# The lower weight parts that fall due while the scan runs, issued behind the scan's work of that step

## The reference, cut to what matters

```python
z, xbc, dt_f, dt_b, q, k, v, gates = split_cols(h @ w_in, IN_SPLITS)
...
seg = a_cum[:, :, :, None] - a_cum[:, :, None]
decay = jnp.exp(jnp.where(lower[:, :, None, None], seg, -jnp.inf)).astype(dtype)
cb = jnp.einsum('bclgn,bcsgn->bclsg', c_c, b_c)
y_diag = jnp.einsum('bclsg,bclsgr,bcsgrp->bclgrp', cb, decay, x_c)
...
y_off = jnp.einsum('bclgn,bcgrpn,bclgr->bclgrp', c_c, h_in, jnp.exp(a_cum).astype(dtype))
...
v = (y * jax.nn.silu(z)).astype(jnp.float32).reshape(b, s, SSD_GROUPS, d // SSD_GROUPS)
...
k, v = jnp.split(mem_n @ w_kv, 2, axis=-1)
```

## Time and profile before

| | |
|---|---|
| median of three runs | 2353.67 us (2353.35 to 2355.12) |
| the profiled execution's own time | 2353.92 us |
| its span, first to last instruction | 2352.1 us |
| busy: TensorE (PE) / its weight loads (PEld) | 2324.1 us / 2014.4 us |
| busy: VectorE (DVE) / ScalarE (ACT) / GpSimd (POOL) | 1636.3 / 1243.7 / 262.4 us |
| chain that ended last: share of PE / DVE / ACT | 93% / 3% / 2% |
| granted TensorE clock | 0.999 |

### The profile page before, as it was taken

How to read it: one execution, slowest core, us unless ns; L and a number is a source line. 1 busy time by engine, 2 the same in 40 slices (tenths; PEclk the granted TensorE clock), 3 DMA queues, 4 the chain that set the end, 5 groups by cost and what they waited for, 6 DMA issues and landing times.

```text
span 2352.1 us, 35281 instructions
## 1 busy us (share of the span) xinstructions
PE 2324.1 (99%) x14088; PEld 2014.4 (86%) x14088; DVE 1636.3 (70%) x2353; ACT 1243.7 (53%) x2026; POOL 262.4 (11%) x208
## 2 busy tenths in 40 slices
PE   8999999999999999999999999999999999999998
PEld 7778778777788888899988899998887888899997
DVE  5698845478865455687785788785677565777784
ACT  7777765346663344455554555554544354555552
POOL 0000000465100100100002200001122201100002
PEclk9999999999999999999999999999999999999999
DMA  6221236324666232233233233223322232333222
GB/s 200 81 73 52 88 103 206 103 95 121 204 214 213 88 118 75 81 116 100 90 99 110 86 119 108 90 81 113 110 64 63 90 117 72 108 108 106 87 76 91
DMA packets 177844, 254.05 MB, mean 108 GB/s; under 512 B 10000, under 2 KB 101392, under 8 KB 177680
## 3 DMA queue, kind: packets, MB, share of 16 engines
q1 hardware_dynamic: 176528, 250.22, 33.1%
q10 hardware_dynamic: 1152, 1.57, 0.2%
HBM read 233.93 MB, written 16.78 MB: 107 GB/s over the span
## 4 chain that ended last, share of the span: by engine, by line
PE 93%; DVE 3%; ACT 2%; issue 1%; DMA 0%; POOL 0%; DVEq 0%; SPq 0%; POOLq 0%
PE bank L1492 92%; DVE wlo L2523 1%; PE bank L1660 1%; ACT whi L1899 0%; PE bank L1683 0%; PE bank L1781 0%; PE bank L1805 0%; DVE T L2531 0%; DVE W L2523 0%; DMA zb<-scr_z 0%; ACT E L2163 0%; DVE bank L2842 0%; DMA raw<-in_w_in 0%; PE bank L1618 0%; DVE xg L2527 0%
## 5 line engine op out<-in xcount | busy, mean ns | idle before, releaser
L1492 PE MATMUL bank<-xopr,shi 128*128 128x256 f32 x3360 | 605.0, 283 | 0.0
L1492 PEld LDWEIGHTS bank<-xopr,shi 128*128 128x128 f32 x3360 | 524.5, 192 | 0.5
L1492 PE MATMUL bank<-xopr,slo 128*128 128x256 f32 x1680 | 475.4, 283 | 0.0
L2523 DVE TENSOR_TENSOR wlo<-raw,whi 128x1024 fp32r<-128x1024 f32 (+2 forms) x286 | 354.6, 1244 | 140.8 <-ACT whi L1899 140.2
L1492 PE MATMUL bank<-xh,whi 128*128 128x512 f32 x1016 | 408.0, 402 | 7.4 <-DVE wlo L2523 7.4
L1492 PE MATMUL bank<-xh,wlo 128*128 128x512 f32 x1016 | 397.5, 391 | 0.0
L1492 PE MATMUL bank<-xl,whi 128*128 128x512 f32 x1016 | 397.2, 391 | 0.0
L1899 ACT ACTIVATE whi<-raw 128x1024 fp32r<-128x1024 f32 (+2 forms) x286 | 292.8, 1031 | 136.1 <-PE bank L1492 121.0
L1492 PEld LDWEIGHTS bank<-xopr,slo 128*128 128x128 f32 x1680 | 322.5, 192 | 0.0
L1492 PEld LDWEIGHTS bank<-xh,whi 128*128 128x128 f32 x1016 | 191.5, 188 | 50.0 <-DVE wlo L2523 8.2
L1492 PEld LDWEIGHTS bank<-xh,wlo 128*128 128x128 f32 x1016 | 191.1, 188 | 41.6
(11 more groups left out here) (398 smaller groups left out, 4320.7 us busy)
## 6 DMA issues: line engine op xcount, KB each, us to landing
raw<-in_w_in SPq DMA_DIRECT2D x92, 512.0 KB, 3.5
quarter<-in_w_ffn_in SPq DMA_DIRECT2D x32, 512.0 KB, 4.5
quarter<-in_ffn_gate SPq DMA_DIRECT2D x32, 512.0 KB, 3.6
quarter<-in_ffn_up SPq DMA_DIRECT2D x32, 512.0 KB, 4.6
raw<-in_ffn_down SPq DMA_DIRECT2D x28, 512.0 KB, 4.2
raw<-in_w_xattn_kv SPq DMA_DIRECT2D x16, 512.0 KB, 4.5
raw<-in_w_kv_mem SPq DMA_DIRECT2D x16, 512.0 KB, 4.9
raw<-in_w_branch_ssd SPq DMA_DIRECT2D x16, 512.0 KB, 4.6
```

The lines of the kernel that those rows point to most:

```text
L1492: return e.matmul(out, l, r, start=start, stop=stop, skip_group_check=skip)
L2523: return e.tensor_tensor(out, a, b, op)
```

## The change

`point()` no longer writes the lower parts of weights while the scan runs. It returns them, and `run_beside` writes them at its own end, behind the generators, so behind the half step of the scan that is written at the same m. In `settle` and `drain` they are written directly behind the point. The other delayed steps keep their place, and outside the scan nothing is different.

```diff
+        behind_scan = [False]
+
         def point():
             due = [d for d in delayed if d[0] == 0]
             delayed[:] = [[d[0] - 1, d[1]] for d in delayed if d[0]]
+            if behind_scan[0]:
+                held = [d[1] for d in due if d[1][0] == "w_lo"]
+                due = [d for d in due if d[1][0] != "w_lo"]
+            else:
+                held = []
             for d in sorted(due, key=lambda d: d[1][0] not in ("w_lo", "s_lo")):
...
+            return held
...
         def run_beside(share):
 
-            point()
+            held = point()
             clock[0] += share
...
                     if next(g[0], "end") == "end":
                         beside.remove(g)
+            for what in held:
+                step(*what)
...
             if g in beside:
                 for _ in g[0]:
-                    point()
+                    for what in point():
+                        step(*what)
                 beside.remove(g)
...
             drain(scan)
+            behind_scan[0] = False
...
         scan = start(ssd(), 3.6)
+        behind_scan[0] = True
```

## The result

| | before | after |
|---|---|---|
| median of 16 executions each | 2353.9 us | 2357.47 us |
| ratio, 95% interval | | 1.0015 (1.0008 to 1.0021) |
| the profiled execution's own time / span | 2353.92 / 2352.1 us | 2357.18 / 2354.9 us |
| mean granted TensorE clock of it | 0.999 | 0.998 |

The changed kernel is 3.6 us slower, inside the 0.2% that I had called hardly measurable, and 0.5 us above my range; with this many executions the interval lies wholly above 1, so the change did make it slower. (One execution of each kernel took over 3800 us; neither moves its median by more than 0.2 us.) The other fifteen executions of the changed kernel go with their mean granted clock: five at 0.999 took 2354.1 to 2355.8 us, ten at 0.998 or 0.997 took 2357.2 to 2360.1 us. Lines of the changed kernel lie 14 further down.

What follows compares the result with a forecast made beforehand. TensorE was taken to bound the scan too, so only its waits could be won or made. Gains of -2.6 and a loss of +2.1 us gave -0.5 us, a median of 2353.2 us, range 2349.5 to 2357.0 us.

Steps and rivals of the forecast that it cites:

- the other moved parts I carry at 0: Remaining moved lower parts: room for 2 to 3 us more in z, so 0; at most 2.1 us a place otherwise.
- place 2: Wait of 1.94 us at 529.68 goes, but the lower part then delays bank 5's mask: -1.1 us, bounds -0.7 and -1.5.
- Place 1: TensorE's waits at 508.06 and 517.58 us for an exponential go: -0.5 and -0.2 us.
- Place 3: Wait of 1.84 us at 590.58 for the last `z_silu` goes, ScalarE is late next: -0.8 us, bounds -0.5 and -1.8.
- The gate: Near 635 us `wlo9` falls behind VectorE's wait for a z tile: +4.35 new wait, -1.21 and -1.00 returned, net +2.1 us.
- the lead is swallowed: Rival, 26%: later events on VectorE, ScalarE or transfers take back every gain, only the loss stays: 2355.8 us.
- slower: Rival, 12%: at the gate with the late z tile, gains gone and neither old wait returned: +4.35 us, 2358.0 us.
- wrong: Profile sign: if waits for E stay near 6.8 us in all, the mask was not what the lower part held up.

Runs made afterwards that it cites:

- only_82_84: Kernel before with only the lower parts of 549.12 and 566.66 us moved behind the scan's half step; median +2.4 us against the kernel before.
- all_but_96: Changed kernel with the lower part of 629.11 us put back ahead of the gate, the other 26 moved; median +1.3 us against the kernel before.
- but_three: Changed kernel with the lower parts of 549.12, 566.66 and 629.11 us put back in their old places; median -0.6 us against the kernel before.
- but_four: Changed kernel with the lower parts of 549.12, 555.66, 566.66 and 629.11 us put back; median -0.75 us against the kernel before.
- only_96: Kernel before with only the lower part of 629.11 us moved, from ahead of the gate to right behind it; median +3.15 us.
- late_89: Kernel before with only the lower part of 603.51 us moved, behind the evictions T; median -1.85 us.
- best: Kernel before with lower parts of 504.38, 514.45, 525.91, 587.86 us held, the second memory's eight loads early, that of 603.51 behind the evictions; median -5.95 us.
- best2: best with 24 lower parts held instead of four, all the change moves but those of 549.12, 566.66 and 629.11 us; -4.9 us against the kernel before.
- best3: best with the lower part of 438.63 us held as well; -6.4 us against the kernel before, 2347.75 us, ratio 0.9973.
- early_late: Kernel before with the second memory's eight loads issued early and the lower part of 603.51 us behind the evictions, none held; median -4.6 us.
- z_only: Kernel before with lower parts moved only for the tiles of z, those of the memory products in place; median +1.6 us.

## Why the prediction was wrong

Its sum was -2.6 + 2.1 = -0.5 us. In the same terms the traces have +0.93 + 2.54 = +3.5 us.

**The step that failed** is "the other moved parts I carry at 0". I had bounded it by TensorE's own need of the tile (room for 2 to 3 us), and no tile in z was late. But a moved lower part also lands in front of something: the next mask, on the other bank, or a state sum. I had worked this out at place 2 and did not repeat it at the other places. By the table of the changed kernel these parts are worth -0.62 (71) + 1.09 (`yt`, 82) + 1.98 (84 and what follows) + 0.20 = +2.65 us. Moved alone, 82 costs 0.72 us and 84 another 1.64 (only_82_84, at z tile 14 and the first key tile). Put back out of the 26 the two give only 1.25 (+1.43 in all_but_96, +0.18 in but_three), because the order without them meets the wait for `HB`; with 83 back too it is 2.33 (-0.90 in but_four). So the prices depend on each other. But_three and but_four still lose 0.4 us between z tiles 12 and 14, where the wait for `yt` at 541 stands; what makes it late was not tried.

**Place 1**, -0.7 us: both waits went, and TensorE had 0.65 us of it.

**Place 2**, -1.1 us with bounds -0.7 and -1.5: -0.37. The start of the `Rr` matmuls on bank 5 went from 532.26 to 529.69, which at the lead of 1.27 us and the 0.54 between the two traces' first tiles is 0.77 us, close to the bound that I gave for a lower part of 2.06 us; that was its length there. The agreement is partly luck: the lower part started 1.3 us earlier than I had drawn (526.58, or 527.1 in the kernel before's time, for 528.4), and TensorE came 1.27 us earlier by place 1, which the working had left out; the two cancel. Then 0.4 was lost right behind, part of it a wait of 0.24 us for `HB`, which also stood behind the lower part and was not in my sum.

**Place 3**, -0.8 us: -0.70; the wait of 1.84 us went, with the wait for ScalarE's exponential next, as foreseen (0.61 us at 593.13).

**The gate**, +4.35 - 1.21 - 1.00 = +2.1 us: without the clock +3.59 - 1.21 - 1.24 = +1.14. The place, the cause and the returns were right. The wait was smaller because TensorE itself came 0.93 us late to the tile. The z tile's load was issued earlier than before (628.38) and took 6.4 us instead of 5.4; in the measure used here it landed 0.2 us later, and 4.35 - 0.93 + 0.17 is the 3.59. So the loss ahead of the gate was in part paid for by a shorter wait at it.

**The clock**, which had no term: +1.40 us at the gate (a tile of 4.54 instead of 3.14 us). My list of what could go wrong left it out. Rows at either level give its size: 3.41 us at half clock are at most 1.7 us, an estimate.

The rival "the lead is swallowed" (26%) named the mechanism of the first part, without saying that the swallowing parts cost by themselves, and with 2355.8 us it stood 1.7 us too low. The rival "slower", 2358.0 us, came closest in time, by another route: it had neither old wait at the gate returned, and both were. What I had written under "wrong" happened: the waits for E stayed at 7 us. But what I had said it would mean, that the mask was not what the lower part held up, is not so: the waits went where the lower part left the mask, and new ones came where it now stands ahead of one.

**Still open.** only_96 is 3.15 us slower by the medians and 1.98 in its profiled execution, which was the fastest of its eleven; a later z tile in the others would do it, but no trace shows it. Five of the changed kernel's executions have the mean clock of the kernel before, 0.999, and are only about 1 us slower than it; from the trace I would have expected 2. Why the z tile's load is issued and lands at such different times where nothing ahead of it was moved (the load was issued 1.0 us earlier in only_96 than before) was not looked into. And why the evictions at 605 us are followed by half clock in three of the thirteen traces that have their idle time and not in the other ten is not explained by anything that differs in those rows.

## What to carry to other kernels

An instruction that is moved out of the way of one critical operation stands in the way of the next one on its engine: write down what is behind it in its new place for every one that moves, not for the places with a wait. Move the few that stand ahead of a wait (here holding four or five of 27 kept a lead, 1.9 us at the fourth key tile with four, and holding the others as well took it back). Where an in-order engine stops for a transfer, look first for what is in front of that transfer on its own queue; here eight loads without urgency cost 1.35 us in the kernel before and 4.0 us in the changed one, where the orders on VectorE that were tried gave 1.85 us (late_89) and 1.35 (the four parts in best).

## What the hardware showed that I had not expected

TensorE's granted clock fell to 0.50 (1.2 GHz) for 3.4 us behind idle time in the middle of a stretch in which it is 98% busy. After a single idle time of 2.9 to 3.3 us between matmuls it fell in all three traces (changed, only_96, all_but_96), once right away and twice about 1.4 us later. At the evictions of 605 us, after two idle times of 1.3 (or 1.4) and 0.3 us that end 1.3 us apart, it fell in three of thirteen. Behind other idle times it did not fall: single ones of 1.5 and 1.6 us (at 529.68 and 590.58 in the kernel before), and pairs that end 2.7 us apart, of 1.2 and 1.0 us (before), 1.4 and 1.0 (only_82_84) and 1.7 and 1.0 (late_89), one trace each. So the sum of the idle time alone does not tell when it falls. In the stretch of half clock, matmuls of 512 columns start 0.43 us apart instead of 0.23. So a wait of some us on the critical engine can cost up to 1.7 us (an estimate, half of 3.41) more than its own length, and whether an execution meets it spreads the times. The kernels without the idle time at 605 us and at the gate (best, best2, best3, early_late) show no such stretch in their traces.

The mean granted clock of an execution has to be read with care. In every trace, that of the kernel before too, the last 3.8 to 7.1 us of the span are at half clock, and this alone moves the mean between 0.9985 and 0.9992: best2's profiled execution is listed with 0.998 and has no other such stretch. A mean listed as 0.999 hardly leaves room for one: no trace with such a stretch has it, not even z_only, whose end is among the shortest (3.8 us).
